# Splitting the first query product around the third tile's norm, and its second low part on another engine

## The chip, the cores and the metric

The kernel runs on one NeuronCore of one Trainium2 chip. The metric is the device time of one execution in microseconds (us), the median of three runs. The engines are TensorE (PE, matmuls; PEld is its loading of the stationary operand), VectorE (DVE), ScalarE (ACT), GpSimd (POOL), and SyncE (SP), which here only issues DMA transfers.

## The reference, cut to what matters

The kernel computes one inference step of a two-layer decoder for 256 prompt tokens and 8 samples of 8 tokens, 320 tokens in all, with a model width of 1024. The change lies where each layer goes from its token mixer to its memory attention:

```
h, s = mixer(x, ...)                       # last step of it: o @ w_out
x = post_norm(x, h, ln_g[l, 0], ln_b[l, 0])
c = memory_cross_attention(x, mem_ks[l], mem_vs[l], xattn_w_q[l], xattn_w_o[l])
...
def post_norm(x, h, g, b):
    z = (DN_ALPHA * x + h).astype(F32)
    mu = jnp.mean(z, axis=-1, keepdims=True)
    var = jnp.mean(jnp.square(z - mu), axis=-1, keepdims=True)
    z = (z - mu) * lax.rsqrt(var + LN_EPS)
    return (z * g.astype(F32) + b.astype(F32)).astype(x.dtype)

def memory_cross_attention(x, mem_k, mem_v, w_q, w_o):
    q = (x @ w_q).reshape(B, T, X_HEADS, X_HEAD_DIM)
    ...
```

It happens twice, once in each of the two layers.

## The kernel before

**Products in three parts.** Every dense product is made of three fp32r matmuls: both operands are split in a high part (a cast to fp32r) and a low part (the value less its high part), and `three` (L1890) adds high times high, high times low and low times high. So each weight chunk of 512 rows by 512 columns (`raw`, one of four slots, loaded by SP) goes through two steps before PE may use it: `split` on ACT (L837) writes `w_hi` (one of three slots), then `split` on DVE (L1257) subtracts and writes `w_lo`. A semaphore counts each step: `loaded`, `w_high`, `w_low`, and `w_used` when PE is done with the chunk, in the order of the chunk numbers.

**Blocks.** A weight of 1024 by 1024 is two blocks of 512 columns, and a block is two chunks (rows 0 to 511, rows 512 to 1023). Here the mixer's output weight is the chunks o0 to o3 and the query weight the chunks q0 to q3; o0 and o1 are the first output block, q0 and q1 the first query block.

**The place of the change.** For the second output block PE runs `block_norm` (L2020). The tokens stand in three tiles: tiles 0 and 1 are the prompt (128 rows each), tile 2 the 64 sample tokens. PE makes the products of tile 0, of tile 1, transposes the normed tile 0, makes the products of tile 2, transposes tile 1 (`turn`, L2013), does 18 filler matmuls (`keep_busy`, L2005: their result is not used), waits for the norm of tile 2 and transposes it, does 5 more fillers, and waits until tile 2's transposed low part is there. Then `dense` makes the first query block (L1953, through `three`, so line L1895): each of the 8 row steps, 4 output groups and 3 parts is one matmul with 128 by 128 weights stationary and all 320 tokens moving, 48 matmuls for each chunk.

**Around PE.** For each tile DVE does, in this order: the residual add (L1287, and L1291 for tile 2), statistics (L1300, L1317, L1318), the subtraction and gain (L1321), and the scale and bias (L1324), which sets `ln_done`. ACT makes the reciprocal deviation in between (L871, L873). A transposed tile goes out of PSUM in halves: ACT writes `xt_hi` (L894), DVE `xt_lo` (L1347). In `block_norm` DVE does the halves of tile 0 behind tile 1's norm, and those of tiles 1 and 2 behind tile 2's norm. ACT's order in `layer_norm` is the same.

**The low part of q0 is made by GpSimd** (`split_query`, L756: the same subtraction), since DVE is full of norms at that time. It runs behind the memset L797. Those of q1 to q3 are made by DVE behind the norm. The query block's result goes to PSUM banks 0 to 3; the transposes of tile 0 use banks 0 and 1, those of tile 1 banks 2 and 3, those of tile 2 bank 7.

**After it** SP loads the memory keys into the slots that q0 to q3 free, in order, each load behind `w_used` (L473), and the attention follows.

Of the kernel before, what the change touches and what calls it, by code (L numbers as in the profile page):

```python
# [25 lines left out]
P = 128  # L26
# [3 lines left out]
PROMPT = 256  # L30
SAMPLES, SAMPLE_T = 8, 8
NT = PROMPT + SAMPLES * SAMPLE_T
TILES = 3
# [12 lines left out]
GCH = 24  # L46
# [192 lines left out]
def decoder_step(nc, a):  # L239
    with ExitStack() as ctx:  # L240
# [359 lines left out]
        def _(pool):  # L600
# [168 lines left out]
            for l in range(LAYERS):  # L769
# [25 lines left out]
                for b in range(3):  # L795
                    pool.wait_ge(s0_out[b], 16 * states_all(l, b))
                nc.gpsimd.memset(st_att["qs"][:], 0.0).then_inc(at_z, 1)  # L797
                split_query(chunk_no(first_block(l) + IN_BLOCKS[l] + 2), groups)
                load_ln(3 * l + 1)
                for t in range(TILES):  # L800
                    pool.wait_ge(ln_done, TILES * (3 * l + 1) + t + 1)
# [20 lines left out]
        def _(act):  # L822
# [71 lines left out]
                    nc.scalar.activation(xt_hi[:, per * half:per * (half + 1), t * P:t * P + n],  # L894
                                         ps[:, turn_bank0(u, t) + half, :].rearrange("p (k s) -> p k s", s=n), ACT.Copy).then_inc(xt_h, 1)

            def layer_norm(q, u, moe=False):

                def rows_hi(t):
                    act.wait_ge(ln_done, TILES * q + t + 1)  # L900
                    nc.scalar.activation(st_moe["xn_hi"][:, t, :], x[:, t, :], ACT.Copy).then_inc(mo[q // 3]["xh"], 1)
                tile_rstd(q, 0)
                tile_rstd(q, 1)
                if u:
                    turned(u, 0)
                if moe:
                    rows_hi(0)
                tile_rstd(q, 2)
                if u:
                    turned(u, 1)  # L910
                    turned(u, 2)
                if moe:
                    rows_hi(1)
                    rows_hi(2)
# [88 lines left out]
            for l in range(LAYERS):  # L1003
# [66 lines left out]
                head_norm(l, H - 1)  # L1070
                split_ahead(db, groups)
                split_ahead(db + 1, groups, 3)
                layer_norm(3 * l, 2 + 3 * l)
                act.wait_ge(at_z, l + 1)
                t_ = st_att
                for c in range(2):
# [170 lines left out]
        def _(dve):  # L1247
# [102 lines left out]
            def block_norm(db, groups, q, u):  # L1350

                par = db % 2
                for t in range(TILES):
                    if t < 2:
                        dve.wait_ge(ln_tile, 2 * (q - q // 3) + t + 1)
                    else:
                        dve.wait_ge(w_used, at(chunk_no(db) + 2, groups, GCH))
                    ins = add_tile(db, t, 1)
                    if t == 2:
                        ins.then_inc(evac[par], 1)  # L1360
                        dve.wait_ge(evac[par], db // 2 + 1)
                    else:
                        link(ins)
                    link(tile_stats(t, 1))
                    tile_norm(q, t)
                    if t == 1:
                        turned(u, 0)
                turned(u, 1)
                turned(u, 2)

            def inverse(t):
# [48 lines left out]
            for l in range(LAYERS):  # L1420
# [206 lines left out]
                head_out(H - 1)  # L1627
                add_block(db, groups, 4)
                block_norm(db + 1, groups, 3 * l, 2 + 3 * l)
                splits[0] += 1  # L1630
                dve.wait_ge(w_low, at(splits[0], groups, GCH))
                split_ahead(db + 1, groups)
                t_ = st_att
# [253 lines left out]
        def _(pe):  # L1887
# [38 lines left out]
                if last == 4:  # L1926
                    ins.then_inc(w_used, 1)

            def dense(db, groups, mode, tiles=TILES):

                par = db % 2
                if db >= 2:
                    pe.wait_ge(evac[par], db // 2)
                for half in range(2):
                    k = chunk_no(db) + half
                    if k == 0:
                        pe.wait_ge(xt_l, 6)
                    else:
                        pe.wait_ge(w_low, at(k + 1, groups, GCH))
                    if k == 1:  # L1940
                        pe.wait_ge(xt_l, 8)
                    r, rh = slot_of(k), hi_slot(k)
                    for kc in range(4):
                        kt = 4 * half + kc
                        if k == 0:
                            pe.wait_ge(first_low if kc < 3 else w_low, kc + 1 if kc < 3 else 1)
                        start, stop = kt == 0, kt == KT - 1
                        if db < KV_BLOCKS[0]:
                            ins = memory_products(db, r, rh, kc, kt)
                        elif mode == "T":  # L1950
                            for n in range(4):
                                cols = slice(n * P, (n + 1) * P)
                                ins = three(ps[:, 4 * par + n, 0:NT], w_hi[:, rh, kc, cols], w_lo[:, r, kc, cols],  # L1953
                                            xt_hi[:, kt, 0:NT], xt_lo[:, kt, 0:NT], start, stop, True)
                        else:
                            for t in range(tiles):
                                ins = tile_products(par, r, rh, kc, kt, t)
                    ins.then_inc(w_used, 1)
# [41 lines left out]
            def keep_busy(count, bank):  # L2000
# [3 lines left out]
                for n in range(count):  # L2004
                    mm(ps[:, bank, :].rearrange("p (a c) -> p a c", a=4), rows, rows.unsqueeze(1).to_broadcast([P, 4, P]), start=True, stop=True)  # L2005

            def turn(q, u, t):

                pe.wait_ge(ln_done, TILES * q + t + 1)
# [2 lines left out]
                for kt in range(KT):  # L2012
                    ins = nc.tensor.transpose(ps[:, (0, 2, 7)[t] + kt // per, (kt % per) * n:(kt % per + 1) * n], x[0:n, t, kt * P:(kt + 1) * P], ident[0:n, 0:n])  # L2013
                    if kt % per == per - 1:
                        ins.then_inc(xt_ps, 1)
                if t == 2:
                    keep_busy(5, 5 if q % 3 < 2 else 4)
                    pe.wait_ge(xt_l, turns(u, t) + 1)

            def block_norm(db, groups, q, u):  # L2020
# [3 lines left out]
                turn(q, u, 0)  # L2024
                tile_block(db, groups, 2)
                turn(q, u, 1)
                keep_busy(18 if q % 3 == 0 else 20, 7)
                turn(q, u, 2)

            def transpose_in(u, src, tiles, kts):  # L2030
                for kt in kts:
# [147 lines left out]
            for l in range(LAYERS):  # L2179
# [62 lines left out]
                db = last  # L2242
                second_half(db, groups, (8 * l, VB))
                block_norm(db + 1, groups, 3 * l, 2 + 3 * l)
                dense(db + 2, groups, "T")
                dense(db + 3, groups, "T")
                pe.wait_ge(evac[db % 2], db // 2 + 2)

# [308 lines left out]
```

## Time and profile before

| | |
|---|---|
| median of three runs | 1392.79 us (1392.18 to 1393.89) |
| the profiled execution | 1392.58 us |
| its span, first to last instruction | 1390.8 us |
| mean granted TensorE clock | 0.996 of full speed |
| busy: PE, DVE, ACT, POOL | 1341.8, 1019.4, 756.2, 149.5 us |

The span is what the views of the profile cover; 1.8 us of the execution's time lie outside it. A row of a timeline gives the start, the time to the end of the last of the merged instructions, engine, line, operation and operands; the bracket tells how long the engine sat idle before and what ended that. Durations of PE rows overlap, since matmuls are pipelined: the distance between starts is what one costs.

### The profile page before, as it was taken

The numbers are of one execution on the slowest core, as the hardware profiler recorded it, in microseconds if no ns is written. First come the engines' busy times: TensorE is split into PE (matmuls) and PEld (weight loads), VectorE is DVE, ScalarE is ACT, GpSimd is POOL, SyncE is SP. The second block draws the span as 40 slices with busy tenths as digits, with TensorE's granted clock in tenths as the row PEclk, the third lists the DMA queues.
The fourth block names the chain that finished last, engine by engine and source line by source line (L and its number), as shares of the span: only waits on it lengthen the run. The fifth ranks groups of instructions, "written<-read, shape, count | busy, mean of one in ns | idle before, by whom it ended". The sixth has DMA issues, their size and how long they took to land.

```text
span 1390.8 us, 19714 instructions
## 1 busy us (share of the span) xinstructions
PE 1341.8 (96%) x7671; PEld 1114.8 (80%) x7671; DVE 1019.4 (73%) x1100; ACT 756.2 (54%) x775; POOL 149.5 (11%) x211
## 2 busy tenths in 40 slices
PE   8999999999898999999999999999899999999996
PEld 6798997788676888888887798779777788888884
DVE  4546757763578988898887356782658989898986
ACT  4444623423425876767676353332534777677765
POOL 5200246210000000000000014220000000000000
PEclk9999999999999999999999999999999999999998
DMA  9784454437964999999994455444983799999981
GB/s 284 246 269 151 150 170 138 134 124 262 371 232 155 362 360 338 352 349 348 342 359 141 134 188 178 133 161 175 372 320 131 283 368 336 356 343 342 358 319 38
DMA packets 102002, 353.67 MB, mean 254 GB/s; under 512 B 6368, under 2 KB 32496, under 8 KB 72224
## 3 DMA queue, kind: packets, MB, share of 16 engines
q1 hardware_dynamic: 97056, 336.09, 67.4%
q0 software_dynamic: 4864, 16.45, 3.5%
q8 instruction: 56, 0.92, 0.3%
q14 instruction: 26, 0.21, 0.0%
HBM read 332.85 MB, written 19.67 MB: 253 GB/s over the span
## 4 chain that ended last, share of the span: by engine, by line
PE 81%; DVE 8%; ACT 4%; DMA 3%; POOL 2%; issue 2%; SPq 0%; DVEq 0%; ACTq 0%; POOLq 0%
PE ps L1895 65%; DMA att_kt<-in_cache_mem_v 2%; PE ps L2263 1%; PE ps L2473 1%; PE ps L2286 1%; DVE mix_s L1604 1%; PE ps L2274 1%; PE ps L1904 1%; PE ps L1903 1%; PE ps L2005 1%; DVE x L1324 1%; DVE x L1321 1%; PE ps L2095 1%; PE ps L2416 1%; PE ps L2417 1%
## 5 line engine op out<-in xcount | busy, mean ns | idle before, releaser
L1895 PE MATMUL ps<-w_hi,xt_hi 128*128 128x512 f32 x576 | 229.6, 399 | 5.9 <-DVE w_lo L1261 2.2
L1257 DVE TENSOR_TENSOR w_lo<-raw,w_hi 128x2048 fp32r<-128x2048 f32 x62 | 141.5, 2294 | 125.4 <-ACT w_hi L837 125.4
L1895 PE MATMUL ps<-w_hi,xt_lo 128*128 128x512 f32 x576 | 225.5, 391 | 0.0
L1895 PE MATMUL ps<-w_lo,xt_hi 128*128 128x512 f32 x512 | 200.4, 391 | 0.0
L837 ACT ACTIVATE w_hi<-raw 128x2048 fp32r<-128x2048 f32 x64 | 121.7, 1913 | 143.7 <-PE ps L1895 58.0
L1261 DVE TENSOR_TENSOR moe_lo<-moe_in_raw,w_hi 128x2048 fp32r<-128x2048 f32 x72 | 164.2, 2290 | 22.6 <-ACT w_hi L844 22.6
L1261 DVE TENSOR_TENSOR w_lo<-raw,w_hi 128x2048 fp32r<-128x2048 f32 x72 | 164.8, 2291 | 16.6 <-ACT w_hi L844 16.2
L844 ACT ACTIVATE w_hi<-moe_in_raw 128x2048 fp32r<-128x2048 f32 x72 | 138.1, 1918 | 56.4 <-PE ps L1895 56.4
L844 ACT ACTIVATE w_hi<-raw 128x2048 fp32r<-128x2048 f32 x72 | 137.5, 1912 | 14.8 <-PE ps L1895 14.8
L1895 PE MATMUL ps<-xt_hi,w_hi 128*128 128x320 f32 x448 | 138.6, 309 | 0.2
L1895 PE MATMUL ps<-xt_hi,w_lo 128*128 128x320 f32 x448 | 138.4, 309 | 0.0
L1895 PE MATMUL ps<-xt_lo,w_hi 128*128 128x320 f32 x448 | 138.4, 309 | 0.0
L1895 PEld LDWEIGHTS ps<-w_hi,xt_hi 128*128 128x128 f32 x576 | 108.3, 188 | 32.1 <-DVE w_lo L1257 3.9
L1895 PEld LDWEIGHTS ps<-w_hi,xt_lo 128*128 128x128 f32 x576 | 108.1, 188 | 24.2
L1895 PEld LDWEIGHTS ps<-w_lo,xt_hi 128*128 128x128 f32 x512 | 96.3, 188 | 19.7
L1895 PEld LDWEIGHTS ps<-xt_hi,w_hi 128*128 128x128 f32 x448 | 84.1, 188 | 1.2 <-issue 0.6
L1895 PEld LDWEIGHTS ps<-xt_lo,w_hi 128*128 128x128 f32 x448 | 84.1, 188 | 0.1
L1895 PEld LDWEIGHTS ps<-xt_hi,w_lo 128*128 128x128 f32 x448 | 84.1, 188 | 0.0
L1895 PE MATMUL ps<-w_hi,moe_ht_hi 128*128 128x512 f32 x192 | 77.0, 401 | 0.0
L1895 PE MATMUL ps<-w_hi,moe_ht_lo 128*128 128x512 f32 x192 | 76.1, 396 | 0.0
L1895 PE MATMUL ps<-moe_lo,moe_ht_hi 128*128 128x512 f32 x192 | 76.0, 396 | 0.0
L1895 PE MATMUL ps<-moe_lo,xt_hi 128*128 128x512 f32 x192 | 75.5, 393 | 0.0
(408 smaller groups left out, 2574.0 us busy)
## 6 DMA issues: line engine op xcount, KB each, us to landing
raw<-in_moe_w_gate SPq DMA_DIRECT2D x48, 1024.0 KB, 5.0
moe_in_raw<-in_moe_w_down SPq DMA_DIRECT2D x48, 1024.0 KB, 4.9
moe_in_raw<-in_moe_w_up SPq DMA_DIRECT2D x32, 1024.0 KB, 5.6
raw<-in_moe_w_up SPq DMA_DIRECT2D x32, 1024.0 KB, 5.6
raw<-in_hgrn_w_in SPq DMA_DIRECT2D x16, 1024.0 KB, 5.5
raw<-in_cache_mem_k SPq DMA_DIRECT2D x16, 1024.0 KB, 6.0
moe_in_raw<-in_moe_w_gate SPq DMA_DIRECT2D x16, 1024.0 KB, 5.8
raw<-in_moe_w_down SPq DMA_DIRECT2D x16, 1024.0 KB, 4.9
```

The source lines that it names most:

```text
L837: nc.scalar.activation(hi_at(hi_slot(k)), raw_at(r), ACT.Copy).then_inc(w_high, 1)
L844: nc.scalar.activation(hi_at(j % MH), raw_at(j % MR), ACT.Copy).then_inc(w_high, 1)
L1257: nc.vector.tensor_tensor(lo_at(slot_of(k)), raw_at(slot_of(k)), hi_at(hi_slot(k)).bitcast(F32), ALU.subtract).then_inc(w_low, 1)
L1261: nc.vector.tensor_tensor(lo_at(j % MR), raw_at(j % MR), hi_at(j % MH).bitcast(F32), ALU.subtract).then_inc(w_low, 1)
L1321: link(nc.vector.scalar_tensor_tensor(out=xt, in0=xt, scalar=mean_var[0:n, t, 0:1], in1=ln_gb[0:n, 0, :], op0=ALU.subtract, op1=ALU.mult))
L1324: nc.vector.scalar_tensor_tensor(out=xt, in0=xt, scalar=rstd[0:n, t:t + 1], in1=ln_gb[0:n, 1, :], op0=ALU.mult, op1=ALU.add).then_inc(ln_d ...
L1604: ins = nc.vector.scalar_tensor_tensor(out=s0, in0=s0, scalar=m["dc"][:, h, NCH + b:NCH + b + 1], in1=ps[:, 4 + f % 2, j * V:(j + 1) * V], ...
L1895: ins = mm(out, lhs, rhs, start=start and n == 0, stop=stop and n == 2, skip_group_check=shared)
L1903: mm(ps[0:64, 4 * par + 2, :], xt_hi[:, kt, PROMPT:NT], w_lo[:, r, kc, :], start=False, stop=False)
L1904: ins = mm(ps[:, 4 * par + 2, :], xt_hi[:, kt, PROMPT:TILES * P], w_hi[:, rh, kc, :], start=start, stop=stop)
L2005: mm(ps[:, bank, :].rearrange("p (a c) -> p a c", a=4), rows, rows.unsqueeze(1).to_broadcast([P, 4, P]), start=True, stop=True)
L2095: ins = mm(ps[32 * c:32 * c + 32, 5, r * V:(r + 1) * V], m["e"][:, 2, h, toks], m["states"][h % 3][:, 4 * r + c, :], start=True, stop=True)
```

## The change

In both layers, for the norm ahead of the query product only:

- PE: behind the transposes of tile 1 come 4 fillers instead of 18, then a wait for tile 1's low part, then the first three row steps of q0 for the 256 prompt columns, then the transposes of tile 2, the fourth row step for the prompt columns (in place of the 5 fillers), the wait for tile 2's low part, and the four row steps of q0 for the 64 sample columns. `dense` then does only q1 of this block.
- DVE: the low halves of tile 1 are written ahead of tile 2's residual add.
- ACT: the high halves of tile 1, and the high part of chunk q1, come ahead of tile 2's reciprocal deviation.
- GpSimd: makes the low parts of q0 and of q1, and DVE skips both.

```diff
 # GpSimd
                 nc.gpsimd.memset(st_att["qs"][:], 0.0).then_inc(at_z, 1)
-                split_query(chunk_no(first_block(l) + IN_BLOCKS[l] + 2), groups)
+                for half in range(2):
+                    split_query(chunk_no(first_block(l) + IN_BLOCKS[l] + 2) + half, groups)
                 load_ln(3 * l + 1)
 # ACT, layer_norm
+                if q % 3 == 0:
+                    turned(u, 1)
+                    split(splits[0], groups)
+                    splits[0] += 1
                 tile_rstd(q, 2)
                 if u:
-                    turned(u, 1)
+                    if q % 3:
+                        turned(u, 1)
                     turned(u, 2)
 # DVE, block_norm
+                    if q % 3 == 0 and t == 2:
+                        turned(u, 1)
                     ins = add_tile(db, t, 1)
...
-                turned(u, 1)
+                if q % 3:
+                    turned(u, 1)
                 turned(u, 2)
...
-                splits[0] += 1
+                splits[0] += 2
                 dve.wait_ge(w_low, at(splits[0], groups, GCH))
 # PE
-            def dense(db, groups, mode, tiles=TILES):
+            def dense(db, groups, mode, tiles=TILES, halves=(0, 1)):
...
+            def query_products(db, groups, kts, first, last):
+
+                k = chunk_no(db)
+                pe.wait_ge(w_low, at(k + 1, groups, GCH))
+                for kt in kts:
+                    for n in range(4):
+                        cols = slice(n * P, (n + 1) * P)
+                        ins = three(ps[:, 4 * (db % 2) + n, first:last], w_hi[:, hi_slot(k), kt, cols], w_lo[:, slot_of(k), kt, cols],
+                                    xt_hi[:, kt, first:last], xt_lo[:, kt, first:last], kt == 0 and first == 0, False, True, True)
+                return ins
 # PE, turn
-                if t == 2:
+                if t == 2 and q % 3:
                     keep_busy(5, 5 if q % 3 < 2 else 4)
                     pe.wait_ge(xt_l, turns(u, t) + 1)
 # PE, block_norm
                 turn(q, u, 1)
-                keep_busy(18 if q % 3 == 0 else 20, 7)
-                turn(q, u, 2)
+                if q % 3 == 0:
+                    keep_busy(4, 7)
+                    pe.wait_ge(xt_l, turns(u, 1) + 2)
+                    query_products(db + 1, groups, range(0, 3), 0, PROMPT)
+                    turn(q, u, 2)
+                    query_products(db + 1, groups, range(3, 4), 0, PROMPT)
+                    pe.wait_ge(xt_l, turns(u, 2) + 1)
+                    query_products(db + 1, groups, range(0, 4), PROMPT, NT).then_inc(w_used, 1)
+                else:
+                    keep_busy(20, 7)
+                    turn(q, u, 2)
 # PE, main
-                dense(db + 2, groups, "T")
+                dense(db + 2, groups, "T", halves=(1,))
```

## Rows read from the trace of the kernel before

**Rows 1.** The page: shares of the chain that ended last.
```profile
PE 81%; DVE 8%; ACT 4%; DMA 3%; POOL 2%; issue 2%; SPq 0%; DVEq 0%; ACTq 0%; POOLq 0%
```
**Rows 2.** The chain in order of time, both layers (start, us, what).
```profile
297.44 28.44 PE ps L1895 x192
...
938.38 28.44 PE ps L1895 x192
```
**Rows 3.** Timeline of PE, layer 0.
```profile
289.16 1.09 PE L2013 MATMUL ps<-ident,x 128*128 128x128 f32 x8
290.01 4.35 PE L2005 MATMUL ps<-r_hi 128*128 128x512 f32 x18
295.31 0.71 PE L2013 MATMUL ps<-ident,x 64*128 64x64 f32 x8 [0.95 <-DVE x L1324]
...
297.44 0.42 PE L1895 MATMUL ps<-xt_hi,w_hi 128*128 128x320 f32 x1
```
**Rows 4.** Timeline of DVE, layer 0.
```profile
289.02 1.28 DVE L1347 TENSOR_TENSOR xt_lo<-ps,xt_hi 128x512 fp32r<-128x512 f32 x2
290.22 0.67 DVE L1287 SCALAR_TENSOR_TENSOR x<-x,ps 64x512 f32<-64x512 f32 x1
...
292.68 1.27 DVE L1321 SCALAR_TENSOR_TENSOR x<-x,mean_var,ln_gb 64x1024 f32<-64x1024 f32 x1
293.98 1.28 DVE L1324 SCALAR_TENSOR_TENSOR x<-x,rstd,ln_gb 64x1024 f32<-64x1024 f32 x1
295.29 2.10 DVE L1347 TENSOR_TENSOR xt_lo<-ps,xt_hi 128x512 fp32r<-128x512 f32 x3
```
**Rows 5.** Timeline of ACT, layer 0.
```profile
273.91 1.92 ACT L837 ACTIVATE w_hi<-raw 128x2048 fp32r<-128x2048 f32 x1 [1.97 <-PE ps L1904]
...
296.06 0.60 ACT L894 ACTIVATE xt_hi<-ps 128x512 fp32r<-128x512 f32 x1 [1.88 <-PE ps L2013]
296.56 3.71 ACT L837 ACTIVATE w_hi<-raw 128x2048 fp32r<-128x2048 f32 x2
```
**Rows 6.** Timeline of POOL, layer 0: the low part of q0.
```profile
276.00 4.61 POOL L756 TENSOR_TENSOR w_lo<-raw,w_hi 128x2048 fp32r<-128x2048 f32 x1 [5.14 <-ACT w_hi L837]
```
**Rows 7.** Timeline of DVE, earlier in layer 0.
```profile
178.48 2.47 DVE L1257 TENSOR_TENSOR w_lo<-raw,w_hi 128x2048 fp32r<-128x2048 f32 x1 [0.23 <-ACT w_hi L837]
...
204.73 1.96 DVE L1562 TENSOR_TENSOR w_hi<-mix_v,w_hi 32x1024 fp32r<-32x1024 f32 x1
206.70 1.34 DVE L1563 TENSOR_TENSOR w_hi<-mix_v,w_hi 32x1024 fp32r<-32x1024 f32 x1
```
**Rows 8.** Timeline of POOL over the same stretches.
```profile
178.77 2.45 POOL L728 TENSOR_TENSOR mix_e<-mix_e,mix_bwd 128x128 f32<-128x128 f32 x1
181.18 0.40 POOL L728 TENSOR_TENSOR mix_e<-mix_e,mix_fwd 128x128 f32<-128x128 f32 x1
...
203.72 1.89 POOL L765 TENSOR_TENSOR w_hi<-w_hi,mask 96x1024 fp32r<-96x1024 f32 x1
```
**Rows 9.** Timeline of PE and its weight loads, layer 1: matmuls narrower than 320 columns.
```profile
886.27 0.97 PEld L2121 LDWEIGHTS ps<-own_rows,mix_os 128*128 128x128 f32 x8
...
901.95 0.64 PE L2140 MATMUL ps<-w_hi 96*128 96x256 f32 x4
902.43 0.39 PE L1904 MATMUL ps<-w_hi,xt_hi 128*128 128x512 f32 x1
```
**Rows 10.** Windows: stretch, length, busy time of PE, PEld, DVE, ACT, POOL (instructions), granted clock, DMA share, GB/s.
```profile
903.00:907.10 4.10, 2.02 (x10) 1.07 (x8) 3.43 (x5) 2.68 (x3) 0.00 (x0) 1.00 0.52 172
...
1378.00:1379.00 1.00, 0.12 (x1) 0.00 (x0) 1.00 (x3) 0.97 (x3) 0.00 (x0) 1.00 0.00 0
...
1380.00:1381.00 1.00, 0.00 (x0) 0.00 (x0) 0.96 (x2) 1.00 (x3) 0.00 (x0) 0.77 0.00 0
```
**Rows 11.** Timeline of PE at the kernel's start.
```profile
1.65 3.62 PE L2159 MATMUL ps<-ident 128*128 128x512 f32 x4 [1.65 <-POOLq L614]
...
5.98 1.02 PE L2159 MATMUL ps<-ident 128*128 128x512 f32 x2
```

More of the change, by code:

```diff
@@ L895, in turned, with layer_norm @@
                                          ps[:, turn_bank0(u, t) + half, :].rearrange("p (k s) -> p k s", s=n), ACT.Copy).then_inc(xt_h, 1)
-            def layer_norm(q, u, moe=False):
+            def layer_norm(q, u, moe=False, groups=None):
                 def rows_hi(t):
@@ L1072, in _ @@
                 split_ahead(db + 1, groups, 3)
-                layer_norm(3 * l, 2 + 3 * l)
+                layer_norm(3 * l, 2 + 3 * l, groups=groups)
                 act.wait_ge(at_z, l + 1)
@@ L1933, in dense @@
                     pe.wait_ge(evac[par], db // 2)
-                for half in range(2):
+                for half in halves:
                     k = chunk_no(db) + half
@@ L1953, in dense @@
                                 ins = three(ps[:, 4 * par + n, 0:NT], w_hi[:, rh, kc, cols], w_lo[:, r, kc, cols],
-                                            xt_hi[:, kt, 0:NT], xt_lo[:, kt, 0:NT], start, stop, True)
+                                            xt_hi[:, kt, 0:NT], xt_lo[:, kt, 0:NT], start, stop, True, len(halves) == 1)
                         else:
```

## The prediction, made before the changed kernel was run

> **What bounds the kernel now.** I read the page first: PE carries 81% of the chain that ended last and DVE 8% [rows 1]. The kernel is a queue of matmuls with holes in it, and only what PE waits for costs time. Then the chain in order of time: each layer's query products (192 matmuls, 28.44 us, so 0.148 us each) are on it without a gap [rows 2], so whatever moves their start or length moves the end one for one. Last I read the timelines of the four engines over one such place, layer 0 from 288 to 299 us, to see who ends each wait.
>
> PE transposes tile 1 at 289.16, runs fillers, and waits for the norm of tile 2 before 295.31; the query product starts at 297.44, behind tile 2's low part [rows 3]. DVE is busy all the while: the low halves of tile 0 from 289.02, the residual add of tile 2 at 290.22, its norm from 292.68, done at 295.26 [rows 4]. So between 290.01 and 297.44 PE makes nothing that is used, and DVE's queue is what bounds it. Layer 1 has the same picture, 28.44 us from 938.38 [rows 2]. The first chunk of the query product, q0, takes 48 x 0.148 = 7.1 us and ends at 304.55. The question is when q0 ends after the change; q1 to q3 follow unchanged.
>
> **The change, step by step (layer 0, times in us).**
>
> *ACT.* The transposes of tile 1 are issued from 289.16 to 290.01 [rows 3], so their first half is out at about 289.8. ACT takes 0.60 for a half and starts its next instruction 0.50 after it [rows 5]: high halves ready at 290.4 and 290.9. Then the high part of q1: its slot is free since the third tile's products (289.3), it takes 1.92 [rows 5], so 290.8 to 292.7.
>
> *DVE.* The low halves of tile 1 now stand ahead of the add of tile 2. They can't start before ACT's first half at 290.4 and take about 0.6 each (1.28 for a pair) [rows 4], so tile 2's add starts at 291.6, not 290.22: 1.4 late. Its subtraction L1321 would come 2.46 behind the add, at 294.1 [rows 4].
>
> *GpSimd.* The low part of q1 starts when ACT is done. For q0 that was 276.00 after an ACT end of 275.83 [rows 5, 6], 0.17 later; here 292.9. It takes 4.61 [rows 6], so to 297.5. DVE saves 2.3 us of work behind the norm that nobody waited for.
>
> *The two together.* L1321 has both tensor inputs in SBUF (x and the gain), and so has the subtraction on GpSimd. The trace has such pairs. GpSimd's L765 ran from 203.72 to 205.61 [rows 8]; DVE's L1562 was issued at 204.73 and took 1.96, ending at 206.69, where its twin L1563 took 1.34 [rows 7]. It ended 1.08 behind GpSimd's end: it had waited for all of it. The other way round, L728 took 2.45 instead of 0.40 [rows 8] while DVE's L1257 ran (178.48 to 180.95) [rows 7]. So they exclude each other, and who comes second waits for the whole of the first. In the kernel before, q0's low part on GpSimd (276.00 to 280.61) ended before the first L1321 of the norms; the new one doesn't. With GpSimd first at 292.9 and L1321 at 294.1, DVE waits to 297.5, finishes L1321 1.1 later (298.6), L1324 takes 1.28: the norm of tile 2 is done at 299.9 instead of 295.26. Of these 4.6, 1.4 come from the order on DVE and 3.2 from the wait.
> The Trainium skill speaks against the change here (SBUF — State Buffer, on the shared port pair): a DVE instruction with two SBUF inputs and a GpSimd one that reads SBUF take the pair as an exclusive lock, whoever starts first. By that rule the sum is the one below; without it, it would be the second rival's. The trace agrees, with the 1.96 and the 2.45.
>
> *PE.* Four fillers (0.23 each), then a wait to 291.7. A 256-column matmul costs 0.12 (901.95 to 902.43 for four) [rows 9], so the 36 of three row steps end at 296.1. PE then waits for the norm to 299.9: 3.7 us idle. From the transposes to tile 2's low part it is 2.13, as before [rows 3], hence 302.05; the 12 prompt matmuls of the fourth row step (1.44) fit in that. Then come 48 sample matmuls of 64 columns. The trace has none of this form, so bounds: below, by columns alone, 0.148 x 64/320 = 0.03; above, 0.12 as for 256 columns. Nearest is a 32-column matmul with 128 by 128 weights: eight weight loads in 0.97, the last one 0.19 long, so (0.97 - 0.19)/7 = 0.111 each [rows 9]. Narrow matmuls cost their weight load, so I take 0.111: 48 x 0.111 = 5.3, and q0 ends at 307.4 instead of 304.55. That is 2.8 later per layer. Splitting the product is itself dear: 48 x 0.12 + 5.3 = 11.1 against 7.1.
>
> *The clock.* The granted clock was 1.00 over a stretch with 2.08 of idle PE (903 to 907.1); after the last matmul, which ended at 1378.12, it fell during 1380 to 1381 (0.77, half speed from then on) [rows 10], so some 2.5 after it. 3.7 idle lies beyond both. I give a fall even odds in each layer, so one fall in two layers. Its price: at the start PE is at the lower level, four matmuls in 3.62, where a later pair took 1.02 in all (0.9 and 0.5 each) [rows 11], so up to 1.8 lost if the low level lasts that long into the work, nothing if it ends before. The 12 prompt matmuls alone would be 1.4 longer and no longer hidden. I take 1.2 for a fall.
>
> *What else moves.* In time and hidden: q1's low part (297.5 against 307.4); q2's high and low parts (about 303 and 305.4, needed at 314.5); q3's (309.3 and 311.7, needed at 321.6). GpSimd loads the next gain and bias at 300 instead of 295.6, used in the next norm, 90 us later. SP's key loads wait for `w_used` of q0 on and shift with PE, so the attention shifts as a whole. The fillers taken out cost nothing on any path.
>
> **The sum.** 2 layers x 2.8 = 5.6, plus one fall of 1.2: 6.8. The profiled execution took 1392.58, of which 1390.8 are the span and 1.8 lie around it unchanged; 1392.58 + 6.8 = 1399.4. It lies 0.2 below the median of the runs, so against the median 1399.6; I say 1399.5.
>
> **The rivals.**
> 1. *As above: collision and dear narrow matmuls.* Without a fall 1398.4, with one 1399.6, with two 1400.8. Its bounds: two falls of 1.8 and narrow matmuls at 0.12 (+0.9) give 1402.9; no fall, and 0.08 for a narrow matmul, between the bounds, gives 2 x 1.3 = 2.6: 1395.4.
> 2. *No wait of DVE for GpSimd.* If ACT's split is over 1.2 late, L1321 is issued first, and GpSimd waits instead, which hurts nobody: it would end by 301.3, and q1 is wanted at 304. Then the norm is done at 296.7, q0 ends at 298.85 + 5.3 = 304.2, 0.4 earlier per layer: 1392.0, no change. For it: nothing but the 1.2 margin; against it the rows of ACT, where nothing stands between the halves and the split.
> 3. *Narrow matmuls cost their columns.* The Trainium skill's TensorE: Matmul & The Clock Gate (Back-to-back issue gap) has a matmul spaced by its columns and a small floor. As a mechanism of this kernel: 48 x 0.03 = 1.4, q0 ends at 303.5 even with the collision, 1.0 earlier per layer: 1390.7, still inside no change. The 0.111 of 32 columns speaks against it.
> 4. *Both 2 and 3, the side of a gain.* With no collision and cheap narrow matmuls q0 ends at 300.3, 4.3 earlier per layer: 1384.2. It decides once a narrow matmul is below about 0.08 with no wait on DVE (48 x 0.08 = 3.9, so 1.8 earlier per layer, 1389.2).
>
> **How the numbers follow.** What a measurement of this kernel can tell from no change is 0.2%, or 2.8 us. Chances: rival 1, my forecast, 0.83 (of which 0.02 may end inside no change); rival 2 0.09; rival 3 0.04; rival 4 0.04. So slower 0.81, no change 0.14, faster 0.05. The range holds case 1 with its bounds less the corner where all are at the end at once: 1394.8 to 1402.5. That leaves out the rivals' 0.17.
>
> **What the profile of the changed kernel would show.** GpSimd's L756 twice in each layer, the second from about 292.9 for 4.6. L1321 of tile 2 about 4.5 long instead of 1.27, ending 1.1 behind GpSimd: if it is 1.27, the forecast falls to rival 2. Tile 2's transposes at 299.9, with an idle time of some 3.7 before them. 64-column matmuls 0.11 apart; 0.03 would be rival 3. q0's end at 307.4, and the keys' transposes late by the same. A granted clock below 1.00 near 300 in one of the layers. What would make me wrong: a start of GpSimd behind 294.1, a clock that stays low for several us in both layers (past 1403), or a shift that the attention's loads take up.

## The result

The changed kernel took 1415.62 us, the median of four runs (1412.82 to 1416.67), against 1392.49 for the kernel before on the same chip: a ratio of 1.0162, 95% interval 1.0144 to 1.0181. That is 1.6% slower, where I forecast 0.5% slower, and outside the range. The profiled execution took 1416.67 with a span of 1414.9, against 1392.58 and 1390.8.

The page of the kernel after: the chain that ended last, by engine. It answers to [rows 1], and the shares hardly tell anything: PE's grew by one point.
```profile
PE 82%; DVE 8%; ACT 4%; DMA 3%; POOL 2%; issue 1%; SPq 0%; DVEq 0%; ACTq 0%; POOLq 0%
```
The timeline of DVE and POOL in the kernel after, which answers to [rows 4] (the last two rows are of layer 1); lines have moved, L1327 is L1321 of before, L1330 is L1324, and L1353 is L1347.
```profile
290.23 1.29 DVE L1353 TENSOR_TENSOR xt_lo<-ps,xt_hi 128x512 fp32r<-128x512 f32 x2 [0.60 <-ACT xt_hi L895]
291.44 0.67 DVE L1293 SCALAR_TENSOR_TENSOR x<-x,ps 64x512 f32<-64x512 f32 x1
292.23 4.60 POOL L756 TENSOR_TENSOR w_lo<-raw,w_hi 128x2048 fp32r<-128x2048 f32 x1 [12.29 <-ACT w_hi L838]
293.89 4.01 DVE L1327 SCALAR_TENSOR_TENSOR x<-x,mean_var,ln_gb 64x1024 f32<-64x1024 f32 x1
297.94 1.28 DVE L1330 SCALAR_TENSOR_TENSOR x<-x,rstd,ln_gb 64x1024 f32<-64x1024 f32 x1
...
946.44 4.59 POOL L756 TENSOR_TENSOR w_lo<-raw,w_hi 128x2048 fp32r<-128x2048 f32 x1 [12.36 <-ACT w_hi L838]
947.74 4.37 DVE L1327 SCALAR_TENSOR_TENSOR x<-x,mean_var,ln_gb 64x1024 f32<-64x1024 f32 x1
```
Here the forecast is met almost to the digit. L1327 is held until GpSimd's low part is through (292.23 + 4.60 = 296.83) and ends 1.07 behind it, in layer 1 1.08.

The timeline of PE in layer 0 of the kernel after, which answers to [rows 3].
```profile
288.49 1.09 PE L2033 MATMUL ps<-ident,x 128*128 128x128 f32 x8
...
291.58 0.39 PE L1904 MATMUL ps<-xt_hi,w_hi 128*128 128x256 f32 x1 [1.07 <-DVE xt_lo L1353]
...
299.27 0.71 PE L2033 MATMUL ps<-ident,x 64*128 64x64 f32 x8 [3.11 <-DVE x L1330]
299.91 0.39 PE L1904 MATMUL ps<-xt_hi,w_hi 128*128 128x256 f32 x1
...
302.09 0.26 PE L1904 MATMUL ps<-xt_hi,w_hi 128*128 128x64 f32 x1
302.16 0.40 PE L1904 MATMUL ps<-xt_lo,w_hi 128*128 128x64 f32 x1
302.37 0.40 PE L1904 MATMUL ps<-xt_hi,w_lo 128*128 128x64 f32 x1
...
312.18 0.61 PE L1904 MATMUL ps<-xt_hi,w_hi 128*128 128x320 f32 x1
312.60 0.47 PE L1904 MATMUL ps<-xt_lo,w_hi 128*128 128x320 f32 x1
312.86 0.47 PE L1904 MATMUL ps<-xt_hi,w_lo 128*128 128x320 f32 x1
...
318.55 0.31 PE L1904 MATMUL ps<-xt_hi,w_lo 128*128 128x320 f32 x1
318.70 0.31 PE L1904 MATMUL ps<-xt_hi,w_hi 128*128 128x320 f32 x1
```
Read the distances of starts from the transposes of tile 1: those of tile 2 come 10.78 behind them (forecast 10.74), but the first matmul of q1 comes 23.69 behind them, where the forecast had 18.2. The sample matmuls stand 0.21 apart (48 of them from 302.09 to 312.18), not 0.111, and those of q1 that follow stand 0.26 apart, not 0.147, until about 317.6. The windows of the profile say why. The columns are the stretch, its length, busy time of PE, PEld, DVE, ACT, POOL, the granted clock, DMA share and GB/s; the last rows are of layer 1.
```profile
298.00:300.00 2.00, 0.73 (x9) 0.66 (x9) 1.22 (x1) 0.00 (x0) 0.49 (x1) 1.00 0.00 0
300.00:302.00 2.00, 2.00 (x12) 2.00 (x13) 0.69 (x1) 1.98 (x2) 0.64 (x2) 0.65 0.57 166
302.00:304.00 2.00, 2.00 (x12) 2.00 (x10) 1.48 (x1) 0.41 (x1) 0.00 (x0) 0.50 0.97 324
...
314.00:316.00 2.00, 2.00 (x9) 2.00 (x8) 1.59 (x1) 0.38 (x1) 0.00 (x0) 0.50 0.94 369
316.00:318.00 2.00, 2.00 (x10) 2.00 (x10) 0.70 (x1) 0.00 (x0) 0.00 (x0) 0.59 0.28 119
...
918.00:920.00 2.00, 1.86 (x5) 1.49 (x6) 1.20 (x3) 1.15 (x2) 0.00 (x0) 0.60 0.97 236
920.00:922.00 2.00, 2.00 (x7) 1.48 (x6) 1.23 (x3) 2.00 (x2) 1.29 (x1) 0.55 1.05 393
```
The granted clock fell to its lower level (0.50, 1.2 GHz) at about 300.6, behind the 3.11 us for which PE waited, and it stayed there for 17 us, through all the sample matmuls, although PE and its weight load were busy for 2.00 of every 2.00 us. It did the same in layer 1 (0.50 in every window from 954 to 972), where PE waited 3.42 us and the clock fell within the wait. And it fell once more, ahead of the norm of layer 1, just behind a wait of 2.09 us that ended at 918.14, where the kernel before had the same wait and kept 1.00 [rows 10].

The sum in layer 0, from tile 1's transposes to the first copy of a transposed key (ACT at 327.09 before, at 337.25 after): 37.93 became 48.76, so 10.8 longer. Of it: 2.8 as forecast for the collision and the split; 0.7 because the last 12 prompt matmuls took 2.18 at the lower clock and were not hidden; 4.8 for the 48 sample matmuls (10.09 against 5.3); 2.4 for q1's first 5.4 us (0.26 apart for 0.147). Together 10.7. Layer 1: from 942.68 to 992.48 after, from 930.03 to 968.03 before, 11.8 longer; its extra fall ahead of the norm 1.6. Together 24.2. The spans differ by 24.1; the stretches outside these three differ by -0.7, +0.9 and -0.3 us, which cancel.

### The profile page after: what moved, and what is told of

The parts are those of the page before. It is cut to its first block, busy times and chain, and to the rows that moved or that the text cites. A ratio compares the mean times of both kernels' runs of the same rounds, so it can differ in the third digit from the quotient of the medians.

```text
span 1414.9 us, 19836 instructions
## 1 busy us (share of the span) xinstructions
PE 1360.7 (96%) x7729; PEld 1135.5 (80%) x7729; DVE 1021.0 (72%) x1098; ACT 756.3 (53%) x775; POOL 158.1 (11%) x213
## 4 chain that ended last, share of the span: by engine, by line
PE 82%; DVE 8%; ACT 4%; DMA 3%; POOL 2%; issue 1%; SPq 0%; DVEq 0%; ACTq 0%; POOLq 0%
PE ps L1904 66%; DMA att_kt<-in_cache_mem_v 2%; PE ps L2292 1%; PE ps L1913 1%; PE ps L1912 1%; PE ps L2502 1%; PE ps L2315 1%; DVE mix_s L1613 1%; PE ps L2303 1%; DVE x L1327 1%; PE ps L2014 1%; PE ps L2445 1%; PE ps L2446 1%; PE ps L2124 1%; PE ps L2181 1%
## 5 line engine op out<-in xcount | busy, mean ns | idle before, releaser
L1263 DVE TENSOR_TENSOR w_lo<-raw,w_hi 128x2048 fp32r<-128x2048 f32 x60 | 137.0, 2293 | 135.0 <-ACT w_hi L838 135.0
L1267 DVE TENSOR_TENSOR w_lo<-raw,w_hi 128x2048 fp32r<-128x2048 f32 x72 | 164.9, 2292 | 16.6 <-ACT w_hi L845 16.1
L1904 PE MATMUL ps<-xt_hi,w_hi 128*128 128x320 f32 (+2 forms) x480 | 154.1, 321 | 1.9 <-DVE xt_lo L1353 1.9
L1904 PE MATMUL ps<-xt_lo,w_hi 128*128 128x320 f32 (+2 forms) x480 | 153.6, 320 | 0.0
L1904 PE MATMUL ps<-xt_hi,w_lo 128*128 128x320 f32 (+2 forms) x480 | 153.5, 320 | 0.0
L1904 PEld LDWEIGHTS ps<-w_hi,xt_lo 128*128 128x128 f32 x576 | 108.5, 188 | 24.2
L1904 PEld LDWEIGHTS ps<-xt_hi,w_hi 128*128 128x128 f32 x480 | 97.8, 204 | 3.0 <-DVE xt_lo L1353 1.5
L1904 PEld LDWEIGHTS ps<-xt_lo,w_hi 128*128 128x128 f32 x480 | 97.7, 204 | 0.1
L1904 PEld LDWEIGHTS ps<-xt_hi,w_lo 128*128 128x128 f32 x480 | 97.8, 204 | 0.0
```

Of the source, the lines that this page charges most:

```text
L1263: nc.vector.tensor_tensor(lo_at(slot_of(k)), raw_at(slot_of(k)), hi_at(hi_slot(k)).bitcast(F32), ALU.subtract).then_inc(w_low, 1)
L1267: nc.vector.tensor_tensor(lo_at(j % MR), raw_at(j % MR), hi_at(j % MH).bitcast(F32), ALU.subtract).then_inc(w_low, 1)
L1904: ins = mm(out, lhs, rhs, start=start and n == 0, stop=stop and n == 2, skip_group_check=shared)
```

## The experiments

Twelve more kernels ran, and each ratio below is against the kernel before in runs on the same chip. A profile shows one execution only: that of e2 was its fastest (1396.74), those of e5 and e10 were their slowest (1395.44 and 1409.63). Since tile 1's transposes in layer 0 start anywhere from 286.56 to 289.76 in the profiled executions, before anything that the kernels differ in, I compare the stretch from tile 1's transposes to q1's first matmul (320 columns wide), "D" below, in layer 0. Before: 289.16 to 304.58, so 15.42. D ends where q1 begins, so it leaves out what a low clock costs within q1.

| kernel | median, us | ratio, 95% interval | D | windows with a clock below 1.00 (layer 0; layer 1; ahead of layer 1's norm) |
|---|---|---|---|---|
| before | 1392.5 to 1393.1 | 1 | 15.42 | none |
| after | 1415.62 | 1.0162 (1.0144 to 1.0181) | 23.69 | 300-318; 952-974; 918-922 |
| e1, gap filled | 1403.51 | 1.0074 (1.0057 to 1.0091) | 18.31 | 306-310; 950-960; 910-914 |
| e2, no collision | 1399.25 | 1.0048 (1.003 to 1.0065) | 15.91 | 302-308; 944-954; none |
| e3, wide samples | 1404.52 | 1.0079 (1.0062 to 1.0096) | 20.21 | 300-306; 946-954; 912-916 |
| e4, collision alone | 1399.19 | 1.0038 (1.0024 to 1.0053) | 18.61 | none |
| e5, e2 + wide | 1393.70 | 1.0003 (0.9994 to 1.0012) | 16.01 | none; none; 908-914 |
| e6, e1 + wide | 1397.87 | 1.0041 (1.0028 to 1.0055) | 18.77 | none |
| e7, high parts first | 1390.53 | 0.9985 (0.9976 to 0.9994) | 13.84 | none; none; 906-910 |
| e8, e7 + narrow | 1392.13 | 1.0001 (0.9991 to 1.0011) | 13.58 | none; none; 904-910 |
| e9, e7 + filler | 1387.98 | 0.9968 (0.9958 to 0.9978) | 13.84 | none |
| e10, split in place | 1404.74 | 1.0093 (1.0077 to 1.0109) | 20.08 | 308-316; 956-964; 916-920 |
| e11, e10 + wide | 1402.23 | 1.0069 (1.0057 to 1.0082) | 19.88 | none |
| e12, before + filler | 1392.30 | 0.9996 (0.9987 to 1.0005) | 15.42 | none |

### e1: is it the idle gap that costs the clock?

```diff
                     query_products(db + 1, groups, range(0, 3), 0, PROMPT)
+                    keep_busy(14, 7)
                     turn(q, u, 2)
```


> The changed kernel with 14 filler matmuls (3.2 us) put into the gap in which TensorE waits for the norm of tile 2, behind the 36 prompt products; the collision of GpSimd and VectorE stays. Theory 1 (the idle gap lets the clock fall, and the narrow matmuls behind it only keep it low): the clock is 1.00 through the 48 narrow matmuls, they are 0.111 us apart, and the time is that of the collision and the split alone: 2.8 us per layer over the kernel before, 1398 us (1396 to 1400). Theory 2 (a stretch of narrow matmuls lowers the clock by itself, gap or no gap): the clock falls within the narrow stretch and the time stays above 1404 us.

1403.51: 12 us less than after (0.88% by the ratios), between the two theories and nearer to the second. The gap was filled and the fall behind it was gone, but in layer 0 another came just behind the sample matmuls (they ran from 300.39 to 305.73), and in layer 1 one came within them.
```profile
304.00:306.00 2.00, 2.00 (x19) 2.00 (x19) 0.00 (x0) 0.01 (x1) 0.00 (x0) 1.00 0.00 0
306.00:308.00 2.00, 2.00 (x10) 2.00 (x10) 0.07 (x1) 1.90 (x1) 0.00 (x0) 0.57 0.49 82
```
So the gap starts the long fall, and it is not the only thing that lowers the clock.

### e2: the low part of q1 back on DVE

```diff
-                for half in range(2):
-                    split_query(chunk_no(first_block(l) + IN_BLOCKS[l] + 2) + half, groups)
+                split_query(chunk_no(first_block(l) + IN_BLOCKS[l] + 2), groups)
...
-                splits[0] += 2
+                splits[0] += 1
```


> The changed kernel with the second low part given back to VectorE behind the norm (GpSimd makes only the first, as before); everything else of the change stays. Theory 1 (collision makes the gap, the gap makes the low clock): the subtraction of tile 2's norm is 1.27 us long, TensorE waits under 1 us for the norm, the clock stays at 1.00, and each layer is 0.4 us shorter than before: 1392 us (1391 to 1394). Theory 2 (narrow matmuls lower the clock by themselves): clock below 1.00 near 300 us and 1398 us or more. Theory 3 (the order on ScalarE and VectorE, not GpSimd, costs the time): 1400 us or more with the clock at 1.00.

1399.25, and theory 2 holds. L1326 of tile 2 is back to 1.27, PE waits 0.37 for the norm, and still the clock falls. Timelines of DVE and PE and windows of e2, layer 0:
```profile
294.20 1.27 DVE L1326 SCALAR_TENSOR_TENSOR x<-x,mean_var,ln_gb 64x1024 f32<-64x1024 f32 x1
...
296.83 0.71 PE L2032 MATMUL ps<-ident,x 64*128 64x64 f32 x8 [0.37 <-DVE x L1329]
...
299.00 0.26 PE L1903 MATMUL ps<-xt_hi,w_hi 128*128 128x64 f32 x1
...
304.71 0.61 PE L1903 MATMUL ps<-xt_hi,w_hi 128*128 128x320 f32 x1
```
```profile
302.00:304.00 2.00, 2.00 (x20) 2.00 (x20) 1.30 (x1) 0.00 (x0) 0.00 (x0) 0.98 0.01 4
304.00:306.00 2.00, 2.00 (x10) 2.00 (x10) 0.00 (x0) 1.01 (x1) 0.00 (x0) 0.50 0.11 16
306.00:308.00 2.00, 2.00 (x11) 2.00 (x10) 1.07 (x1) 0.90 (x1) 0.00 (x0) 0.66 0.86 258
```
The clock fell at about 304, five us into a stretch of nothing but 64-column matmuls, with no idle time of PE since 296.8. That points to the narrow matmuls themselves, but DVE's and ACT's order differs here too; e10 below settles it. The forecast had no such case. Against after, e2 is one edit and worth 1.14% (16 us), the most of any: it takes away the collision and with it the wait of 3.11.

### e3: the sample matmuls made wide

The 64 sample columns are moved four times over, so that each matmul is 256 wide; the extra copies land in unused columns of the same PSUM banks.
```diff
+                    hi, lo = (x[:, kt, PROMPT:NT].unsqueeze(1).to_broadcast([P, 4, NT - PROMPT]) for x in (xt_hi, xt_lo))
...
-                    query_products(db + 1, groups, range(0, 4), PROMPT, NT).then_inc(w_used, 1)
+                    sample_products(db + 1, groups).then_inc(w_used, 1)
```


> The changed kernel, but each of the 48 sample matmuls moves the 64 sample columns four times over (256 columns, the further three copies go to unused columns of PSUM). More work for TensorE, the same result; collision and gap stay. Theory 1 (narrow matmuls, bound by their weight load, keep the clock low once it has fallen): with wide ones it comes back within some 3.5 us, the stretch takes 7 to 8 us instead of 10.3 and the rest of the first query block runs at full clock, so about 5 us per layer come off: 1405 us (1402 to 1409), although the matmuls are wider. Rival (the clock comes back after a fixed time of some 17 us, whatever runs): no gain, 1415 us or more.

1404.52, as theory 1 had it: matmuls with four times the columns made the kernel 11 us faster. Behind the same wait of 3.11 the clock fell, but in layer 0 it rose again within the wide matmuls (in layer 1 it stayed low for 6.8 us, where after had 20.5):
```profile
300.00:302.00 2.00, 2.00 (x16) 1.93 (x15) 0.69 (x1) 1.77 (x2) 0.85 (x2) 0.82 0.28 106
302.00:304.00 2.00, 2.00 (x11) 2.00 (x11) 1.27 (x1) 0.62 (x1) 0.00 (x0) 0.50 0.96 311
304.00:306.00 2.00, 2.00 (x16) 2.00 (x15) 1.02 (x1) 0.00 (x0) 0.00 (x0) 0.82 0.26 107
```

### e4: the collision alone

The kernel before, with q1's low part on GpSimd, its high part ahead of tile 2's reciprocal deviation on ACT, and 32 fillers for 18.
```diff
-                split_query(chunk_no(first_block(l) + IN_BLOCKS[l] + 2), groups)
+                for half in range(2):
+                    split_query(chunk_no(first_block(l) + IN_BLOCKS[l] + 2) + half, groups)
...
-                keep_busy(18 if q % 3 == 0 else 20, 7)
+                keep_busy(32 if q % 3 == 0 else 20, 7)
```


> The kernel before with one part of the change alone: the second low part on GpSimd, with its high part on ScalarE ahead of tile 2's reciprocal deviation; 32 fillers instead of 18 ahead of tile 2's transposes, so that the clock stays up. Theory 1 (GpSimd and VectorE exclude each other): the subtraction of tile 2's norm ends 1.1 us behind GpSimd, near 297.1 us in layer 0, so the query product starts 3.1 us later in each layer: 1398.7 us (1397 to 1400). Rival (they only share a path and both get somewhat slower, or don't meet): 1393 to 1395 us, with GpSimd's subtraction longer than 4.6 us.

1399.19, as expected; the clock stayed at 1.00, and D grew by 3.2. The timeline of e4, layer 0:
```profile
290.42 4.60 POOL L756 TENSOR_TENSOR w_lo<-raw,w_hi 128x2048 fp32r<-128x2048 f32 x1 [10.86 <-ACT w_hi L838]
291.63 4.47 DVE L1325 SCALAR_TENSOR_TENSOR x<-x,mean_var,ln_gb 64x1024 f32<-64x1024 f32 x1
```
DVE's 4.47 is 3.2 above its 1.27 [rows 4], and that is what the norm, and with it each layer, loses.

### e5 and e6: both covers, without and with the collision

e5 is e2 with e3's wide samples, e6 is e1 with them.

> The kernel e2 (GpSimd makes only the first low part, so no shared work with VectorE), in which now the 48 sample products move the 64 sample columns four times over (256 columns wide; the three further copies land in unused columns of the same PSUM banks). Theory 1 (what e2 lost was the clock, lowered by the stretch of narrow matmuls): the clock stays at 1.00 in every window from 290 to 330 and from 930 to 980 us; the third tile's norm is about 1.9 us later per layer (VectorE does two low parts of the second tile first, 1.29 for both and the waits), the products behind it 48 x 0.12 = 5.8 against 48 x 0.147 = 7.1: about 0.5 us more per layer, 1393 to 1395 us. Theory 2 (the clock is lowered by something else in this order, such as the idle time of TensorE ahead of the prompt products, 1.07 us): a window below 1.00 is still there and the time is over 1396.

> The kernel after with both covers: 14 fillers in the gap ahead of the third tile's transposes (e1) and the widened sample products (e3); GpSimd still makes both low parts. Theory 1 (three causes add up: collision, the gap, the narrow stretch): both clock falls around the change are gone, and only the collision is left, about 3 us per layer on top of what e5 costs: 1399 to 1401.5 us. Rival (the clock also falls for another reason, as it did ahead of the norm of layer 1 in after and e1): 1402 or more, with a window below 1.00 at 908 to 922 us.

e5: 1393.70, no difference from before. With the narrow matmuls gone, 0.45% by the ratios (6 us, 3 a layer) went with them. D is 0.6 longer than before, as worked out. e6: 1397.87, a little below its range; not one window below 1.00 in its profile ahead of the last matmul. Between e6 and e5 lie the collision and the 14 fillers, which only fill the wait that the collision makes: 0.38% or 5.3 us, and 2.76 in D.

### e10 and e11: the split alone, in the order of before

The kernel before with q0 made behind tile 2's low part as always, but as 48 matmuls of 256 columns and then 48 of 64 (e10), or of 64 moved four times (e11).
```diff
                 turn(q, u, 2)
+                if q % 3 == 0:
+                    query_products(db + 1, groups, range(0, 4), 0, PROMPT)
+                    query_products(db + 1, groups, range(0, 4), PROMPT, NT).then_inc(w_used, 1)
...
-                dense(db + 2, groups, "T")
+                dense(db + 2, groups, "T", halves=(1,))
```


> The kernel before in its own order (nothing on VectorE, ScalarE or GpSimd changes, no product ahead of the third tile's norm), only with the first 48 query products each cut in two: 48 of 256 prompt columns, then 48 of 64 sample columns. If narrow products alone lower the clock: a fall within or behind the second 48 in each layer as in e2; 48 x (0.12 + 0.111 - 0.147) = 4.0 us per layer for the cut and 2.5 to 3 per layer for the fall: 1404 to 1408 us. If the clock needs an idle stretch ahead: clock 1.00, 1400 to 1402 us.

> As e10, the sample columns moved four times over (256 wide). Both theories: clock 1.00, 48 x (0.12 + 0.12 - 0.147) = 4.5 us per layer: 1401 to 1402.5 us; by the difference e10 - e11 the price of what narrow products do to the clock is read (expected 4 us or so more for e10, although its products are the shorter ones).

e10 1404.74, e11 1402.23: the kernel with more columns to move is the faster one, though by 0.24% (3.3 us), not the 4 expected. The intervals of the two overlap a little, but all five runs of e10 (1404.14 and up) lie above all six of e11 (1403.00 and down). In e10 the sample matmuls ran from 303.88 to 309.84 in layer 0, and from 953.79 to 961.00 in layer 1, where the clock fell after only 3.2 us of them. Its windows (the last is of layer 1), and then those of e11:
```profile
303.88 0.20 PE L1895 MATMUL ps<-xt_hi,w_hi 128*128 128x64 f32 x1
...
306.00:308.00 2.00, 2.00 (x20) 2.00 (x19) 0.00 (x0) 0.00 (x0) 0.00 (x0) 1.00 0.00 0
308.00:310.00 2.00, 2.00 (x13) 2.00 (x13) 0.00 (x0) 0.00 (x0) 0.00 (x0) 0.61 0.00 0
310.00:312.00 2.00, 2.00 (x9) 2.00 (x9) 0.00 (x0) 1.88 (x1) 0.00 (x0) 0.50 0.28 74
...
953.79 0.20 PE L1895 MATMUL ps<-xt_hi,w_hi 128*128 128x64 f32 x1
...
956.00:958.00 2.00, 2.00 (x15) 2.00 (x15) 0.00 (x0) 0.00 (x0) 0.00 (x0) 0.74 0.00 0
```
```profile
306.00:308.00 2.00, 2.00 (x19) 2.00 (x18) 0.00 (x0) 0.00 (x0) 0.00 (x0) 1.00 0.00 0
308.00:310.00 2.00, 2.00 (x17) 2.00 (x17) 0.00 (x0) 0.97 (x1) 0.00 (x0) 1.00 0.00 0
```
PE had not been idle since 295.9, and DVE and GpSimd had no part in it, so e10 with e11 beside it shows the narrow matmuls as the cause on their own. And splitting q0 into two parts moved 256 wide costs 4.5 us a layer even with the clock up (D 19.88 against 15.42): 48 matmuls of 320 columns take 7.1, 96 of 256 take 11.6.

### e7, e8, e9, e12: a version that gains

The gap can be used without touching DVE's order. Of the three products, two move only high parts, and these are there earlier. So ACT makes tile 1's high halves early (as in after), DVE keeps its order of before and makes q1's low part, tile 1 is transposed into banks 4 and 5, and PE does this (against the kernel after; the comments are put in here):
```diff
                     keep_busy(4, 7)
-                    pe.wait_ge(xt_l, turns(u, 1) + 2)
-                    query_products(db + 1, groups, range(0, 3), 0, PROMPT)
+                    pe.wait_ge(xt_h, turns(u, 1) + 2)
+                    pe.wait_ge(xt_l, turns(u, 0) + 2)
+                    query_high(db + 1, groups, False)      # 32 matmuls: w_hi and w_lo by xt_hi, prompt columns
                     turn(q, u, 2)
-                    query_products(db + 1, groups, range(3, 4), 0, PROMPT)
+                    keep_busy(3, 6)
+                    pe.wait_ge(xt_h, turns(u, 2) + 1)
+                    query_high(db + 1, groups, True)       # 32: sample columns, moved four times
                     pe.wait_ge(xt_l, turns(u, 2) + 1)
-                    query_products(db + 1, groups, range(0, 4), PROMPT, NT).then_inc(w_used, 1)
+                    query_low(db + 1, groups).then_inc(w_used, 1)   # 16: w_hi by xt_lo, all 320 columns
```
e8 leaves the samples 64 wide. e9 (from e7) and e12 (from before) put 9 fillers where layer 1 waits 2.09 us ahead of its norm:
```diff
+                if l == 1:
+                    keep_busy(9, 3)
                 second_half(db, groups, (8 * l, VB))
```


> A version that takes only what the gap can hold without delaying VectorE: low part of q1 on VectorE, its order as in the kernel before; ScalarE rounds the second tile's columns ahead of the third tile's norm; TensorE does, ahead of that norm, the 32 products of the prompt's high columns (w_hi and w_lo by xt_hi, 32 x 0.12 = 3.8 us in place of 18 fillers), behind the third tile's transposes the 32 of the sample columns (widened to 256), and last the 16 of w_hi by xt_lo for all 320 columns; the second tile's transposes go to banks 4 and 5. Theory: behind the third tile's transposes 32 x 0.12 + 16 x 0.147 = 6.2 us from 0.7 behind them, against 7.1 from 1.4 behind them in before: 1.6 us less per layer, 1388.5 to 1391 us, with the clock at 1.00. Rival: the clock falls and the time is 1393 or more.

> As e7, with the 32 sample products left 64 columns wide (32 x 0.111 = 3.6 us). If only a stretch of narrow products as long as e2's 48 (5.3 us) lowers the clock, this gives 0.3 us less per layer than e7: about 1389. If 32 of them are enough to lower it: a window at 0.5 to 0.9 behind them in one or both layers, 1 to 3 us each, 1391 to 1396.

> The kernel e7 with 9 fillers (into bank 3) in layer 1 ahead of the second half of the block in front of the first norm, where TensorE waits 2.09 us on a low part and where the clock fell in e7, e5, e1 and after, not in before. If a fall there costs the 2 us or so that two windows at half clock make: clock 1.00 everywhere, 1388.5 to 1390 us, and fewer runs apart from each other. Rival: the fillers run past the wait or the fall moves elsewhere: as e7, 1390.5 or more.

> The kernel before with the 9 fillers of e9 alone. Its clock did not fall in the profiled run of before; if it does in some of its runs, this one is 0 to 1 us faster and its runs lie closer together (1391.5 to 1393); as control for e9.

e7: 1390.53, ratio 0.9985 with an interval below 1; D is 1.58 shorter, for 1.6 expected. e9: 1387.98, a little better than expected: 0.32% faster than before (0.22% to 0.42%) and the fastest kernel of the study. Its timeline of PE and of DVE in layer 0:
```profile
292.71 0.71 PE L2042 MATMUL ps<-ident,x 64*128 64x64 f32 x8 [0.23 <-DVE x L1329]
...
294.16 0.34 PE L2024 MATMUL ps<-xt_hi,w_hi 128*128 128x256 f32 x1
...
298.05 2.51 PE L2032 MATMUL ps<-xt_lo,w_hi 128*128 128x320 f32 x16
300.40 0.31 PE L1900 MATMUL ps<-xt_hi,w_hi 128*128 128x320 f32 x1
```
```profile
290.08 1.27 DVE L1326 SCALAR_TENSOR_TENSOR x<-x,mean_var,ln_gb 64x1024 f32<-64x1024 f32 x1
...
292.69 2.09 DVE L1352 TENSOR_TENSOR xt_lo<-ps,xt_hi 128x512 fp32r<-128x512 f32 x3
```
PE starts on the samples 1.45 behind tile 2's transposes, and the low part, done at 294.78, is hidden behind them. From e7 to e9 the windows at 906 to 910 went back to 1.00. The intervals of e7 and e9 just overlap, and of the 4.84 us between their profiled executions 2.45 lie ahead of layer 0's tile 1, where the two kernels are the same, so how much of the step the filler makes is not shown. e12, the same filler in the kernel before, changes nothing that can be told: there the clock did not fall in the profiled execution either. e8's profile shows no fall behind its 32 narrow matmuls (3.5 us), but that execution was its fastest (1390.23), with a mean granted clock of 0.996. Its seven runs from 1392.11 to 1395.48 have 0.992 or 0.993, and its four below 1391.7 have 0.994 to 0.996; e7's eleven runs, up to 1392.01, have 0.994 to 0.996. So the clock did fall more in most runs of e8, by an estimate of some 8 to 11 us more at the lower level (0.003 or 0.004 of 1390 us, at half the clock). The only difference between the two kernels is the width of the 32 sample matmuls, so these are the cause, though where in the kernel the clock fell no profile shows. The time, 1392.13, lies in the range that I gave for "32 are enough", and the wide form is the better one.

## Why the prediction was wrong

*ACT, DVE, GpSimd and the two together: right in the sum.* GpSimd started 3.7 behind tile 1's transposes (forecast the same), took 4.60 (4.61), DVE's instruction ended 1.07 behind it (1.08), and tile 2's transposes came at 10.78 (10.74). DVE itself ran 0.5 later than forecast (tile 2's add 2.95 behind tile 1's transposes, for 2.44), which cost nothing, since GpSimd's end set the time. So of the 4.6 by which tile 2's transposes are late, DVE's order makes 1.9 (e2 has them at 8.03, before at 6.15) and the wait 2.7, where I had 1.4 and 3.2. e4, with DVE's order of before, has the wait at its full 3.2, in D and by the ratio 0.38% (5.3 us) in all. The rule of the Trainium skill that I weighed (SBUF — State Buffer, on the shared port pair) holds: DVE's instruction took 4.01 to 4.47 in after and e4 and 1.27 in e2, where DVE makes the low part. Rivals 2 and 4 fall with it. One reading was loose without a price: between 290.01 and 297.44 PE does make something that is used, tile 2's transposes from 295.31 [rows 3].

*Narrow matmuls cost their weight load: right at the full clock.* In e8's profile 32 of them took 3.54 us (296.60 to 300.14), so 0.111 each, and rival 3 falls. The spacing that I gave for it is the one that the Trainium skill (TensorE: Matmul & The Clock Gate, Back-to-back issue gap) has for a matmul by itself; for pairs of weight load and matmul it says that both set the spacing, and the trace agrees with that. The Trainium skill (TensorE: Matmul & The Clock Gate, LDWEIGHTS) prices a weight load by its columns alone, by its formula an estimate of 107 ns for 128, with no other price for a lower clock. The trace agrees at the full clock and not at the half, where the loads and their narrow matmuls stood 0.21 apart.

*The clock: this is the step that failed.* I wrote "one fall in two layers" at 1.2 us, and so 1.2 us in the sum. It cost some 17 us. Three things were wrong in it. The chance: the clock fell in both layers. The price of a fall: I took it from the kernel's start, where wide matmuls follow, and bounded it by 1.8. (That PE is at the lower level there was inferred from matmuls of 0.9 for 0.5 us [rows 11]; the granted clock reads 1.00 in all windows of that stretch.) Here the 48 narrow matmuls followed, and the clock did not rise within them; it rose 5.4 us into the wide ones. So everything from 300.6 to 317.6 ran at half the clock, 7.9 us lost in layer 0. And the cause: I looked for falls only behind idle time. e2 and e10 show the clock falling within a busy stretch of narrow matmuls. Among the signs of being wrong I had named "a clock that stays low for several us in both layers", and that is what came. The idle time itself was close: 3.11 and 3.42 us for 3.7.

By the ratios the 1.62% come apart in more than one way. After to e1 (fill the gap) is 0.88%, e1 to e6 (widen the samples) 0.33%, e6 to e5 (no collision, and no fillers) 0.38%, e5 to before 0.03%; 12.3, 4.6, 5.3 and 0.4 us. Widening first (after to e3) gives 0.83% and filling then (e3 to e6) 0.38%. Taking the collision away first (after to e2) gives 1.14%, since the gap goes with it, and widening then (e2 to e5) 0.45%. The first of the two covers, filler or width, is worth 12 us, whichever it is, and the second 5, because both shorten the same stretch: the gap starts the fall and the narrow matmuls prolong it. With intervals of 0.1% to 0.2% on each side, such a part is exact to some 2 or 3 us only. For the collision D is the sharper measure: 2.76 a layer between e5 and e6, 5.5 in all.

*The splits elsewhere: right.* The low part of q1 was in time, and the shift reached the end of the kernel whole, to within 1 us.

*The extra fall ahead of layer 1's norm (1.6 us): not foreseen, and not settled.* The same wait of 2.08 or 2.09 us was followed by a lower clock in the profiled runs of after, e1, e3, e5, e7, e8 and e10, and by none in those of before, e2, e4, e6 and e11. The wait and the code around it are the same in all. Near the kernel's start, where no edit has acted yet, the clock also fell in some profiled executions: in those of e5, e7 and e10, where PE's wait before 17.6 us was 1.79 to 2.21, and in no other, where it was 0.20 to 1.63. So waits far shorter than the 3.1 of the change can be followed by a fall, and what decides it for one and the same wait stayed open.

## What to carry to other kernels

Before you cut a wide matmul so that a part of it can start earlier, price the parts: with 128-column weights 256 columns cost 0.12 us and 64 cost 0.11, where 320 cost 0.147, so cutting 48 matmuls of 320 costs 4.0 us by these prices (4.5 measured in e11, with both parts 256 wide), about the 4.35 of fillers that it could replace [rows 3]. Price a fall of the clock by the work that follows it, at up to double its time, and not by an average: in the kernel after narrow matmuls didn't bring the clock back, and in e10 a stretch of them took it down. Cut along the operand that is there early (the high parts), keep the last piece full width, and look at what else the helper engine's instruction shares with the one on the critical path.

## What the runs showed of the hardware that I had not expected

- A stretch of 64-column matmuls, each with its own 128-column weight load, was followed by a lower granted clock with PE and PEld busy throughout: 4.6 us behind its start in e10, 4.9 in e2 and 5.9 in e1 (just behind its end) in layer 0, and 3.2, 4.3 and 4.6 in layer 1. In e8, where it lasted 3.5 us, the profiled execution shows none, but seven of eleven runs have a mean clock lower by 0.003 or 0.004. In after the clock stayed at 1.2 GHz for the whole 10 us of it. The same instructions with the columns moved four times over kept 2.4 GHz (e11, e5), at 0.12 for 0.111 us each. Why narrow matmuls lower the clock no run shows.
- At the lower clock a narrow matmul with its weight load took 0.21 us for 0.111, and one of 320 columns 0.26 for 0.147.
- In one and the same place a wait of 2.09 us of PE was followed by the lower clock in seven profiled kernels and not in five others.
